# Splitting the subtraction that makes a weight tile's low part: six blocks on VectorE, two on GpSimd

## The reference

```python
# first block, layer l (mixers: differential attention and a gated recurrence, or dilated attention)
mix = even_mixer(...) if l % 2 == 0 else odd_mixer(...)      # x @ w_in, ..., @ w_out
x = layer_norm(ALPHA * x + mix, ln1_g[l], ln1_b[l])
hdn = jnp.square(jax.nn.relu(x @ ffn_w1[l]))
x = layer_norm(ALPHA * x + hdn @ ffn_w2[l], ln2_g[l], ln2_b[l])
x = x + jax.nn.sigmoid(x @ ple_w_gate[l]) * rms_norm(p[l] @ ple_w_proj[l], ple_norm_g[l])
# second block, layer i, for x and, but for the last parts of layer 1, for xc with the same weights
y, yc = token_mixers(h, hc, w_in[i], w_out[i], ...)           # GLA, neighbourhood and window attention
x = x + g1 * y
x = x + g2 * ((jax.nn.silu(h @ w_gate) * (h @ w_up)) @ w_down)
```

## Time and profile before

| what | value |
|---|---|
| median of 3 runs | 1936.05 us (1930.65 to 1936.8) |
| the profiled execution's own time | 1936.03 us |
| its span in the profile | 1934.7 us |
| PE busy | 1830.1 us, 95% |
| DVE busy | 1268.5 us, 66% |
| ACT busy | 1000.2 us, 52% |
| POOL busy | 77.5 us, 4% |
| TensorE clock granted, mean | 0.979 of full speed |
| making low parts (L541, 520 tiles) | 638.1 us of DVE |
| casting high parts (L533, 520 tiles) | 543.8 us of ACT |

### The profile page before, as it was taken

How to read it: one execution, slowest core, us unless ns; L and a number is a source line. 1 busy time by engine, 2 the same in 40 slices (tenths; PEclk the granted TensorE clock), 3 DMA queues, 4 the chain that set the end, 5 groups by cost and what they waited for, 6 DMA issues and landing times. The chain is left out here.

```text
span 1934.7 us, 35649 instructions
## 1 busy us (share of the span) xinstructions
PE 1830.1 (95%) x14792; PEld 1675.2 (87%) x14792; DVE 1268.5 (66%) x2327; ACT 1000.2 (52%) x1748; POOL 77.5 (4%) x78
## 2 busy tenths in 40 slices
PE   5998899999999989999988999999999989889997
PEld 3775699998888969999988998899999978589997
DVE  3535565667867786666666677776775667756665
ACT  3444443547755565454465565554554455544443
POOL 0000100002000020000020010100100000100000
PEclk9999999999999999999998999999999989989999
DMA  8898875563454425555544444355555533235553
GB/s 320 296 314 296 266 235 188 181 202 113 138 171 131 141 66 166 190 182 190 184 131 156 152 153 132 110 164 185 179 172 172 176 120 110 66 104 181 185 185 120
DMA packets 93824, 334.91 MB, mean 173 GB/s; under 512 B 10960, under 2 KB 12880, under 8 KB 93536
## 3 DMA queue, kind: packets, MB, share of 16 engines
q1 hardware_dynamic: 92016, 327.33, 51.6%
q0 software_dynamic: 1648, 5.31, 0.9%
HBM read 331.55 MB, written 1.05 MB: 172 GB/s over the span
## 5 line engine op out<-in xcount | busy, mean ns | idle before, releaser
L541 DVE TENSOR_TENSOR low<-ring,high 128x1024 fp32r<-128x1024 f32 x410 | 501.5, 1224 | 260.4 <-ACT high L533 257.6
L566 PE MATMUL bank<-XHx,high 128*128 128x256 f32 x2096 | 613.1, 293 | 36.3 <-DVE XLx L647 20.9
L533 ACT CAST high<-ring 128x1024 fp32r<-128x1024 f32 x410 | 428.6, 1045 | 329.9 <-PE bank L568 277.4
L567 PE MATMUL bank<-XLx,high 128*128 128x256 f32 x2096 | 594.9, 284 | 0.0
L568 PE MATMUL bank<-XHx,low 128*128 128x256 f32 x2096 | 594.6, 284 | 0.0
L566 PEld LDWEIGHTS bank<-XHx,high 128*128 128x128 f32 x2096 | 401.8, 192 | 67.5 <-issue 47.1
L567 PEld LDWEIGHTS bank<-XLx,high 128*128 128x128 f32 x2096 | 403.0, 192 | 1.0
L568 PEld LDWEIGHTS bank<-XHx,low 128*128 128x128 f32 x2096 | 403.1, 192 | 0.0
L566 PE MATMUL bank<-XHc,high_side 128*128 128x256 f32 x608 | 181.7, 299 | 13.3 <-DVE low_side L541 11.7
L567 PE MATMUL bank<-XLc,high_side 128*128 128x256 f32 x608 | 172.8, 284 | 0.0
L568 PE MATMUL bank<-XHc,low_side 128*128 128x256 f32 x608 | 172.4, 284 | 0.0
(11 more groups left out here) (448 smaller groups left out, 3078.9 us busy)
## 6 DMA issues: line engine op xcount, KB each, us to landing
ring<-in_stream SPq DMA_DIRECT2D x410, 512.0 KB, 3.6
ring_side<-in_stream SPq DMA_DIRECT2D x110, 512.0 KB, 3.7
ring_mod<-in_stream SPq DMA_DIRECT2D x96, 512.0 KB, 5.4
x_nb<-in_rpb POOLq DMA_DIRECT2D x6, 256.0 KB, 3.3
x_late_NB<-in_rpb POOLq DMA_DIRECT2D x6, 256.0 KB, 3.2
Xx<-in_x SPq DMA_DIRECT2D x2, 512.0 KB, 4.6
Xc<-in_ctx SPq DMA_DIRECT2D x1, 1024.0 KB, 6.5
out<-y SPq DMA_DIRECT2D x8, 128.0 KB, 2.0
```

The lines of the kernel that those rows point to most:

```text
L533: nc.scalar.copy(st.high[:, j % st.n_split, :], st.ring[:, j % st.n_ring, :]).then_inc(*A.tick(st.s_high, A_us(TB * P), (st.name, "high", j)))
L541: nc.vector.tensor_tensor(st.low[:, j % st.n_ring, :], st.ring[:, j % st.n_ring, :], st.high[:, j % st.n_split, :].bitcast(F32), ALU.subtr ...
L566: nc.tensor.matmul(out, wh, xh, start=(i == 0), stop=False)
L567: nc.tensor.matmul(out, wh, xl, start=False, stop=False)
```

## The change

Six of a tile's eight low blocks are still made by VectorE; the last two are made by GpSimd, in a new step `gpsimd_low` with a signal of its own, `low_done_gpsimd`. Both start from the same `high_done`. PE waits for VectorE's signal before the tile's first block as before, and for GpSimd's before the first group of blocks that reaches into the last two. The planner is told 0.95 us for VectorE's part (1.217 before) and 1.0 us for GpSimd's.

```diff
+        self.s_high, self.s_low, self.s_low_pool, self.s_used = (
+            signal(f"{name}_{x}") for x in ("high_done", "low_done", "low_done_gpsimd", "used"))
...
-        nc.vector.tensor_tensor(st.low[:, j % st.n_ring, :], st.ring[:, j % st.n_ring, :],
-                                st.high[:, j % st.n_split, :].bitcast(F32), ALU.subtract).then_inc(
-            *V.tick(st.s_low, V_us(TB * P), (st.name, "low", j)))
+        nc.vector.tensor_tensor(st.low[:, j % st.n_ring, LOW_VECTOR], st.ring[:, j % st.n_ring, LOW_VECTOR],
+                                st.high[:, j % st.n_split, LOW_VECTOR].bitcast(F32), ALU.subtract).then_inc(
+            *V.tick(st.s_low, V_us(6 * P), (st.name, "low", j)))
+
+def gpsimd_low(k, st):
+    nc, G = k.nc, k.G
+    for j in range(MAIN_TILES if st.plan is None else len(st.plan)):
+        G.wait_ge(st.s_high, (yield st.name, "high", j))
+        nc.gpsimd.tensor_tensor(st.low[:, j % st.n_ring, LOW_GPSIMD], st.ring[:, j % st.n_ring, LOW_GPSIMD],
+                                st.high[:, j % st.n_split, LOW_GPSIMD].bitcast(F32), ALU.subtract).then_inc(
+            *G.tick(st.s_low_pool, 1.0, (st.name, "low end", j)))
+
+LOW_VECTOR, LOW_GPSIMD = slice(0, 6 * P), slice(6 * P, TB * P)
...
     if o == 0:
         k.T.wait_ge(st.s_low, (yield st.name, "low", tile))
+    if o + len(blocks) > 6 and o <= 6:
+        k.T.wait_ge(st.s_low_pool, (yield st.name, "low end", tile))
...
+    k.add(G, gpsimd_low(k, k.main), 1)
+    k.add(G, gpsimd_low(k, k.side), 1)
```

## The result

| | before | with the change |
|---|---|---|
| median, runs taken side by side | 1934.57 us (20 runs) | 1937.88 us (20 runs, 1933.87 to 1946.13) |
| ratio | | 1.0021, 95% interval 1.0013 to 1.003 |
| profiled span | 1934.7 us | 1934.8 us |
| low parts on VectorE / on GpSimd | 638.1 us / none | 560.9 us / 645.0 us |

The account below looks back on a forecast made before the run. PE was taken as the bound, busy 1830.1 of 1934.7 us, leaving 104.6 us idle. The terms -6.8 + 2.7 + 2.7 + 1.5 + 1 gave +1.1 us on 1936.03, so 1937 us, range 1926 to 1957.

Parts of the forecast that it names:

- What one instruction costs: Split low parts: VectorE's six blocks 0.96 us; GpSimd's two 0.69 us alone, about 1.65 if begun beside VectorE.
- Relief, -6.8: Shorter low parts on VectorE save PE 3.0 us at direct waits and 3.8 us further back in chains.
- The direct waits: 11 PE waits ended directly by weight tiles' low parts, 14.2 us in all; 0.27 us saved each, 3.0 us.
- My ceiling of 9.2 us: Most relief possible: 83.7 us of PE idle time x 50% low parts' share of VectorE's work x 22% shortening.
- The lock, +5.4: GpSimd and VectorE block each other's SBUF reads: 2.7 us at followers of low parts plus 2.7 us elsewhere.
- The first 2.7 us: Blocked VectorE instructions behind low parts in PE's chains: ten places, half losing the race, 5 x 0.54 us.
- elsewhere on the path the two engines meet by chance: Chance meetings of VectorE and GpSimd in norms, rope and decays: 2.7 us, with 0 and 6 as ends.
- Rival 2: GpSimd's reads block VectorE's chains nearly each time, with clock dips: about +14, 1950 us; chance 0.37 split evenly with rival 3.
- GpSimd's list, +2.5: Low ends queue behind other GpSimd work: 1.5 us at layer norms' biases, 1 us at attention's position biases.
- rival 3: PE waits for GpSimd's low ends stuck behind norm biases or bias loads: 1942 to 1946 us; chance 0.37 split evenly with Rival 2.
- The order, 0 (-3 to +7): The planner's new times reshuffle the lists of PE, ACT, DVE and SP; taken as 0, range -3 to +7 us.
- Clock: Sign of a wrong prediction: PE's mean clock leaves 0.979 by more than 0.003, or its idle total moves over 8 us.

Follow-up runs that it names:

- old_relief: Six low blocks on VectorE, GpSimd fills the other two with zeros, in the instruction order of the kernel before; 1927.07 us, ratio 0.9959 to that kernel.
- order_only: The change's order and signals, but VectorE makes all eight blocks and GpSimd only clears four scratch columns; 1939.71 us, ratio 1.0023 to the kernel before.
- relief_only: The change's order with six blocks on VectorE, but GpSimd fills the other two with zeros; 1927.4 us, ratio 0.9957 to the kernel before.
- old_order: The change's real split, six blocks on VectorE and two on GpSimd, in the instruction order of the kernel before; 1938.22 us, ratio 1.0016 to that kernel.
- one_input: As old_order, but GpSimd reads one SBUF tensor instead of two, multiplying raw blocks by 0; 1931.22 us, ratio 0.9988 to the kernel before.
- vector_first: As old_order, but GpSimd's part waits for VectorE's signal, not ScalarE's; 1928.43 us, ratio 0.9972 to the kernel before; repeated, 1929.71 us, 0.998.
- change_vector_first: The change's lists word for word, but GpSimd's part waits for VectorE's low_done instead of high_done; 1932.11 us, ratio 1.0004 to the kernel before.

## Why the prediction was right, and where it was not

The forecast was 1937 us, no change; the result is a ratio of 1.0021, or +3.3 us where the sum said +1.1. The sign of the sum was right and its size off by 2.2 us. That much agreement is luck: the relief was too small by 1.5 to 5.5 us, the price of the two engines' meeting too small by about 6, and the 2.5 us for GpSimd's list were not seen at all. The errors have both signs and cancel.

1. **What one instruction costs: right.** VectorE's part is 0.96 us in the median, as worked out. GpSimd's is 0.72 to 0.74 us alone, where I had 0.69; beside VectorE it is 1.51, not 1.65: in the meeting shown above only 0.6 us of it lie behind VectorE's end, less than its bare 0.74.
2. **Relief, -6.8: too small.** It is 8.3 us in before's order. The direct waits went as said: from 14.2 us to 11.1 in old_relief, 3.1 us where the sum had 3.0. My ceiling of 9.2 us took a shortening of 22% off half of PE's idle time, and in the change's order 12.3 us came. The ceiling left out busy time. Between the profiled spans of before and old_relief lie 9.2 us, and only 6.5 of them are idle time; between order_only and relief_only they are 16.4 and 5.9. The rest is matmuls that start closer together.
3. **The lock, +5.4: half of what it is.** The mechanism and the price of one meeting were right: up to 0.54 us for a follower and 0.27 net for PE; measured, 0.53 (0.95 - 0.42) and 0.26, at the very place of the earlier trace rows. The first 2.7 us came out near right, from two errors. I had ten places and half of them lost. PE waits for `x_hidden_low` at only four, and all four lost the race: compared matmul by matmul with old_relief, old_order is 0.53 us later at each, 2.1 us together. ("Half of them to lose the race" is wrong besides: 84 of 99 lose it in the change.) What failed is the other 2.7 us, "elsewhere on the path the two engines meet by chance". By the measured 11.2 us some 9 lie there. Three waits for a norm's sum (RSx L1759, 0.53 us each) have 1.6 of them, waits for side tiles' low parts 2.5, and those for the context path's normed chunks 1.9. The side tiles' share was in no term of the sum, which let VectorE's own part go undisturbed: GpSimd holds up 127 of the 520, which takes 62 us of the 140 us of relief away again. (These shares are of the 16.0 us between the two profiled spans. Of the same, 2.4 lie in the wait at the start and 4.7 at transfers of `ring_mod`, which differ that much between any two profiles here.) The places of the rest are too scattered to name.
4. **The rule of the Trainium skill.** That every pair would be serial is what two-operand pairs do here: 108 low parts over 1.4 us, 318 GpSimd parts over 1.4. The Trainium skill ("SBUF — State Buffer", section "SBUF: two separate sides") says that the first comer holds the ports for its whole instruction, and the trace agrees, by 1.53 beside 0.74 us and 0.96 beside 1.50. With one operand on GpSimd it doesn't agree: in one_input VectorE's part takes 1.19 us behind a GpSimd instruction of 0.85 that began 0.02 us earlier. The section doesn't say who is next when both engines go on asking. By the start alone the meeting cost 11 us (old_order) or 1 to 4 (vector_first, twice, against old_relief).
5. **Rival 2's point of decision was reached, and the time didn't follow.** I had put it at a mean blocking of 0.27 us for each tile. It was 0.28: relief_only has VectorE busy for 1137.2 us, the change for 1284.9, and the difference over 520 is 0.28. Yet the kernel is 3 us slower, not 14, because the relief, which rival 2 left at 6.8, pays for most of it. Such a point must set both terms against each other.
6. **GpSimd's list, +2.5: nothing seen.** The biases do stand between low ends near 450 us (four of them in one piece, 5.6 us in the change and 5.9 in order_only), but no wait of PE names GpSimd's part in the change. The cover of 18 x 0.118 = 2.1 us held, so rival 3 is out for this kernel. (Its sum was off too: 3 us at three or four norms and 4 at the heads are 13 to 16 us, not 10 to 14.) In change_vector_first it came true once, for 2.75 us.
7. **The order, 0 (-3 to +7): within its range.** +4 us with full low parts, about 0 with short ones.
8. **Clock.** The mean was 0.985 and not within 0.003 of 0.979, which I had named as a sign of being wrong. It wasn't one: PE's idle total moved by less than 1 us (105.3 against 104.6), and the spans are equal. The clock's mean differs by that much between profiles of kernels of equal time (0.980 for old_relief, 0.984 for relief_only), so my bound was too tight.

## What to carry to other kernels

Before a VectorE instruction is split with GpSimd, look at what follows it on VectorE: if that reads two SBUF tensors and someone waits for it, a GpSimd part released by the same signal was served before it in 84 of 99 cases here, and most of its length (0.53 of 0.74 us) is what the follower pays. Where GpSimd begins first, VectorE's own part pays too. Release GpSimd's part by VectorE's own completion instead, if the consumer has the slack, and put it into GpSimd's list in VectorE's order. And measure relief and contention apart (here by filling with zeros): a result near zero was a gain of 8 to 12 us and a loss of 11 to 12.

## What the runs showed of the hardware

- When VectorE and GpSimd meet with two SBUF operands each, the one that is already waiting seems to be served at the next handover, even if the other has its next instruction right behind: 330 of 520 GpSimd parts at 1.5 us and the follower at 0.80 us on average in old_order, 19 of 520 and 0.49 in vector_first, where GpSimd begins about 0.1 us after VectorE's end. The durations show who ran first; the handover itself is my reading.
- Filling SBUF with zeros on GpSimd, 0.31 us for 128 x 256, delays nothing on VectorE (other work 728 us, 726 before).
- A GpSimd instruction with one SBUF operand does delay VectorE, by 0.15 us on L1303 where two operands do by 0.38, though it is itself longer (1.37 us on average against 1.25). Where it began first and took 0.85 us, VectorE's part took 1.19 us, 0.23 more than its bare 0.96.
- On the same amount of work per engine, the start of GpSimd's part changed the kernel by 37 us (1970.33 and 1933.72, with four blocks each).
